# Half-length Fourier transform on folded rows, a rotation table built during the projection, and Toeplitz loads moved behind it

## What is computed

```
h = rms_norm(x, g_pre_mix) * (1 + sc_m) + sh_m
u, f, q, k, v = split(h @ w_in)
y_ssm = s5_mixer(u, ...)      # two complex linear scans, forward and backward, then GELU and a gate
y_fft = fourier_mixer(f, w_fft)
y_att = window_attention(q, k, v, sink)
y = concat(y_ssm, y_fft, y_att) @ w_out

def fourier_mixer(f, w_fft):
    ff = f.reshape(bsz, seq, FFT_HEADS, HEAD_DIM)
    mixed = fft2(ff, axes=(1, 3), norm='ortho').real
    return einsum('bshd,hde->bshe', mixed, w_fft)
```

## Time and profile before

| | |
|---|---|
| median of 3 runs | 3597.83 us |
| the three runs | 3597.83, 3578.83, 3598.26 us |
| profiled execution | 3580.67 us, its span 3578.9 us |
| PE busy | 3307.5 us (92% of the span) |
| DVE busy | 1477.8 us (41%) |
| ACT busy | 1020.0 us (29%) |
| mean granted TensorE clock | 0.963 of full speed |

### The profile page before, as it was taken

The page is one execution under the profiler, slowest core; times in us unless marked ns, Lnnn a source line. Parts: engine busy times, 40 slices in busy tenths (PEclk is TensorE's granted clock), DMA queues, the critical chain, the costliest instruction groups (busy, mean ns, idle before and its releaser), DMA issues.

```text
span 3578.9 us, 37529 instructions
## 1 busy us (share of the span) xinstructions
PE 3307.5 (92%) x14497; PEld 2571.8 (72%) x14497; DVE 1477.8 (41%) x2617; ACT 1020.0 (29%) x1475; POOL 217.8 (6%) x251
## 2 busy tenths in 40 slices
PE   6999788799999999999999998966888899999997
PEld 2575466688888788788888886754446688888885
DVE  6523642733443334411112354898543611111355
ACT  1111333523322232311121332314542312111231
POOL 4100210000000000000000001113330000000000
PEclk9899899899999999999999999987999999999998
DMA  8232003311111243211112343101003311111242
GB/s 279 96 58 100 11 8 112 100 47 47 47 52 48 76 135 119 81 53 47 47 47 65 108 132 96 36 24 34 1 0 113 117 47 47 49 51 47 94 141 100
DMA packets 245610, 260.35 MB, mean 73 GB/s; under 512 B 25680, under 2 KB 187464, under 8 KB 245396
## 3 DMA queue, kind: packets, MB, share of 16 engines
q1 hardware_dynamic: 235736, 253.05, 22.6%
q10 hardware_dynamic: 9788, 6.16, 0.6%
HBM read 237.55 MB, written 21.34 MB: 72 GB/s over the span
## 4 chain that ended last, share of the span: by engine, by line
PE 81%; DVE 10%; issue 4%; ACT 3%; ACTq 1%; DMA 0%; SPq 0%; POOL 0%; DVEq 0%
PE psum L942 40%; PE psum L797 25%; PE psum L2411 2%; PE psum L2440 2%; PE psum L1662 2%; DVE count_junk L1865 2%; PE psum L291 2%; PE psum L1642 1%; PE psum L1562 1%; PE psum L366 1%; DVE p L1930 1%; PE psum L335 1%; PE psum L1508 1%; PE psum L1652 1%; ACTq L2046 1%
## 5 line engine op out<-in xcount | busy, mean ns | idle before, releaser
L942 PE MATMUL psum<-x_hi,split_hi 128*128 128x512 f32 x2112 | 661.6, 391 | 14.7 <-DVE x_lo L1214 14.7
L942 PE MATMUL psum<-x_lo,split_hi 128*128 128x512 f32 x2112 | 660.7, 390 | 0.0
L942 PE MATMUL psum<-x_hi,split_lo 128*128 128x512 f32 x2112 | 660.3, 390 | 0.0
L942 PEld LDWEIGHTS psum<-x_hi,split_hi 128*128 128x128 f32 x2112 | 398.2, 189 | 99.5 <-DVE x_lo L1214 16.8
L942 PEld LDWEIGHTS psum<-x_hi,split_lo 128*128 128x128 f32 x2112 | 398.0, 188 | 82.9
L942 PEld LDWEIGHTS psum<-x_lo,split_hi 128*128 128x128 f32 x2112 | 398.1, 188 | 82.8
L797 PE MATMUL psum<-split_hi,src_hi 128*128 128x512 f32 x1312 | 406.6, 391 | 19.6 <-DVE split_lo L767 12.4
L797 PE MATMUL psum<-split_lo,src_hi 128*128 128x512 f32 x1312 | 405.5, 390 | 0.0
L797 PE MATMUL psum<-split_hi,src_lo 128*128 128x512 f32 x1312 | 405.1, 390 | 0.0
L848 DVE TENSOR_TENSOR split_lo<-raw,split_hi 128x1024 fp32r<-128x1024 f32 x132 | 160.8, 1220 | 564.4 <-ACT split_hi L844 564.4
L844 ACT CAST split_hi<-raw 128x1024 fp32r<-128x1024 f32 x132 | 138.7, 1052 | 604.5 <-PE psum L942 595.9
(11 more groups left out here) (393 smaller groups left out, 3594.5 us busy)
## 6 DMA issues: line engine op xcount, KB each, us to landing
raw<-in_ffn_w SPq DMA_DIRECT2D x176, 512.0 KB, 3.7
ada_w<-in_w_ada SPq DMA_DIRECT2D x12, 2048.0 KB
raw<-in_w_up SPq DMA_DIRECT2D x44, 512.0 KB, 3.7
raw<-in_w_down SPq DMA_DIRECT2D x44, 512.0 KB, 3.5
raw<-in_w_out SPq DMA_DIRECT2D x32, 512.0 KB, 3.5
res_dram<-hidden SPq DMA_DIRECT2D x32, 512.0 KB, 4.1
hidden<-res_dram SPq DMA_DIRECT2D x32, 512.0 KB, 5.2
dft_w<-in_dft SPq DMA_DIRECT2D x16, 512.0 KB, 3.7
```

Of the source, the lines that this page charges most:

```text
L942: ins = t.matmul(bank(4 * par + 2 * u + half), l[u][:, cols], r[:, k, HALF * half:HALF * (half + 1)], start=(k == 0 and m == 0), stop=(k = ...
```

## The change

1. **SP's order.** The eight loads `toep` move from ahead of units 4 to 9's loads to behind the Fourier tables and `att_bias`, where they wait for `uc_turned` (their new place is that of `u_rows`). `turn[0]` moves to the old place of `toep`.
2. **Folding.** Rows n and 1024-n of `f` meet the same cosine and opposite sines. `fold_fourier` on DVE, behind `split(4)`, writes their sum in the lower half of `f_t` and their difference in the upper half (six operations of 511 elements). Row 512 stands alone (`f_mid`).
3. **Mixing with `fw`.** Four blocks instead of eight, each by four 128-column matmuls instead of two of 256, and two with one output row for `f_mid`.
4. **Transform over positions.** The tables have 512 rows and 512 columns: four loads instead of 16, 16 matmuls of 512 columns instead of 64, even part and odd part in banks of their own. Two matmuls with one weight row (`dft_alt`) add row 512, and ten of two columns (`dft_alt_cols`) make output position 512. ACT copies the two odd banks, DVE adds and subtracts (the subtraction is written in reverse order).
5. **`turns(0)`** moves on DVE behind `split(5)`, in smaller pieces (at most 256 elements instead of 384). `turns(1)` stays, without the wait for `uc_turned`.

```diff
-    toep = place("toep", [P, CH, GROUPS * GC], RR + 16 * KB)
+    toep = place("toep", [P, CH, GROUPS * GC], RR)
...
-    turn = [place("turn", [P, 2, PAIRS, NCH], RR)[:], carry[1][:, :, :, 0:NCH]]
+    turn = [place("turn", [P, 2, PAIRS, NCH], RR + 16 * KB)[:], carry[1][:, :, :, 0:NCH]]
...
         sp.wait_ge(win_mm, Z_ALL)
-        for i in range(2 * NT):
-            if i >= 4:
-                sp.wait_ge(dft_mm, i - 3)
-            sp.dma_start(dft_w[i % 4][:], a["dft"][P * (i // 2):P * (i // 2 + 1), i % 2, :]).then_inc(dft_in[i % 4], 16)
+        for i in range(4):
+            sp.dma_start(dft_w[i][:], a["dft"][P * i:P * (i + 1)]).then_inc(dft_in[i // 2], 16)
+        sp.dma_start(dft_alt[:], a["dft_alt"]).then_inc(dft_in[1], 16)
+        sp.dma_start(dft_alt_cols[:], a["dft_alt_cols"]).then_inc(dft_in[1], 16)
         sp.wait_ge(u_turned, 6)
         sp.dma_start(att_bias[:], a["att_bias"]).then_inc(bias_in, 16)
+        sp.wait_ge(uc_turned, 6)
+        for s in range(CH):
+            sp.dma_start(toep[GC * s:GC * (s + 1), :, :],
+                         toep_dram[7 - s:15 - s].rearrange("t c n -> c t n")).then_inc(toep_in, 16)
...
         pe.wait_ge(fw_ready, 1)
-        for n in range(NT):
+        pe.wait_ge(f_folded, 1)
+        for n in range(4):
             if n >= 2:
                 pe.wait_ge(fm_ready, n - 1)
             for pair in range(2):
-                ins = t.matmul(bank(4 + n % 2, 2 * P, 2 * P * pair), f_t[:, pair, P * n:P * (n + 1)],
-                               fw[:, pair].rearrange("p c e -> p (c e)"), start=True, stop=True)
+                for cs in range(2):
+                    at_n = HALF * cs + P * n
+                    ins = t.matmul(bank(4 + n % 2, P, P * (2 * pair + cs)), f_t[:, pair, at_n:at_n + P], fw[:, pair, cs, :],
+                                   start=True, stop=True)
             ins.then_inc(fm_mm, 1)
+        pe.wait_ge(fm_ready, 3)
+        for pair in range(2):
+            ins = t.matmul(bank(4, P, P * pair)[0:1], f_t[:, pair, HALF:HALF + 1], fw[:, pair, 0, :], start=True, stop=True)
+        ins.then_inc(fm_mm, 1)
...
-            for pair in range(2):
-                for half in range(2):
-                    ins = t.matmul(bank(2 * pair + half), f_mixed[:, n, pair, cs, :], dft_w[i % 4][:, HALF * half:HALF * (half + 1)],
-                                   start=(i == 0), stop=(i == 2 * NT - 1))
-            ins.then_inc(dft_mm, 1)
-        pe.wait_ge(yf_ready, 4)
+                for cs in range(2):
+                    t.matmul(bank(2 * pair + cs), f_mixed[:, n, pair, cs, :], dft_w[n][:, cs, :],
+                             start=(n == 0), stop=(n == 3 and cs == 1))
+        for pair in range(2):
+            t.matmul(bank(2 * pair), f_mid[:, pair, :], dft_alt[:], start=False, stop=True)
+        for pair in range(2):
+            for n in range(4):
+                t.matmul(bank(6, 2, 2 * pair), f_mixed[:, n, pair, 0, :], dft_alt_cols[:], start=(n == 0), stop=False)
+            ins = t.matmul(bank(6, 2, 2 * pair), f_mid[:, pair, :], dft_alt_cols[0:1, :], start=False, stop=True)
+        ins.then_inc(dft_mm, 1)
+        pe.wait_ge(yf_ready, 3)
...
+        act.wait_ge(dft_mm, 1)
+        for pair in range(2):
+            s.copy(yf_odd[:, pair, :], bank(2 * pair + 1)).then_inc(yf_odd_ready, 1)
...
+            step = max(x for x in (3, 4, 6, PAIRS) if x * w <= (3 if d else 2) * NCH)
...
+    def fold_fourier(dve, v, steps):
+
+        dve.wait_ge(z_ready, Z_F)
+        for pair in range(2):
+            low, high, back = f_t[:, pair, 1:HALF], f_t[:, pair, HALF + 1:SEQ], f_t[:, pair, HALF + 1:SEQ][:, ::-1]
+            steps.add(v.tensor_tensor(f_diff[:, 1:HALF], low, back, ALU.subtract))
+            steps.settle()
+            steps.add(v.tensor_tensor(low, low, back, ALU.add))
+            steps.settle()
+            steps.add(v.tensor_copy(high, f_diff[:, 1:HALF]))
+            steps.settle()
+        dve.sem_inc(f_folded, 1)
...
+        for pair in range(2):
+            dve.wait_ge(yf_odd_ready, pair + 1)
+            even, odd = bank(2 * pair), yf_odd[:, pair, :]
+            steps.add(v.tensor_tensor(yc_t[:, 3 + pair, 0:HALF], even, odd, ALU.add))
+            ins = v.tensor_tensor(yc_t[:, 3 + pair, HALF + 1:SEQ][:, ::-1], even[:, 1:HALF], odd[:, 1:HALF], ALU.subtract)
+            ins.then_inc(yf_ready, 1)
...
-        sp.wait_ge(k_in_dram, 16 * 15)
-        for s in range(CH):
-            sp.dma_start(toep[GC * s:GC * (s + 1), :, :],
-                         toep_dram[7 - s:15 - s].rearrange("t c n -> c t n")).then_inc(toep_in, 16)
         for n in range(4, len(win_units)):
             sp.wait_ge(win_lo, n - 1)
             load_unit(n)
+        sp.wait_ge(k_in_dram, 16 * 15)
...
         for n in range(3, len(win_units)):
             split(n)
+            if n == 4:
+                fold_fourier(dve, v, steps)
+            elif n == 5:
+                turns(v, steps, 0)
```

More of the change, by code:

```diff
@@ L180, in body @@
     fw = place("fw", [P, 2, 2, P], RR + 42 * KB)
-    f_mixed = place("f_mixed", [P, NT, 2, 2, P], XR + 32 * KB)
-    dft_w = [place(f"dft_w{i}", [P, SEQ], XR + 4 * KB * i) for i in range(4)]
+    f_mixed = place("f_mixed", [P, 4, 2, 2, P], XR + 32 * KB)
+    f_mid = place("f_mid", [1, 2, P], XR + 40 * KB)
+    dft_w = [place(f"dft_w{i}", [P, 2, HALF], XR + 4 * KB * i) for i in range(4)]
+    dft_alt = place("dft_alt", [1, HALF], XR + 16 * KB)
+    dft_alt_cols = place("dft_alt_cols", [P, 2], XR + 18 * KB)
+    yf_odd = place("yf_odd", [P, 2, HALF], XR + 28 * KB)
+    f_diff = place("f_diff", [P, HALF], RR + 10 * KB)
     u_rows = place("u_rows", [P, GROUPS, CH, GC], RR)
@@ L199, in body @@
     probs = [place(f"probs{i}", [P, SPAN], at) for i, at in enumerate(probs_at)]
-    turn_tmp = [place(f"turn_tmp{i}", [P, 3, NCH], XR + 20 * KB + 1536 * i) for i in range(4)]
+    turn_tmp = [[place(f"turn_tmp{d}_{i}", [P, n], at + 4 * n * i) for i in range(4)]
+                for d, (n, at) in enumerate(((2 * NCH, RR + 8 * KB), (3 * NCH, XR + 20 * KB)))]
     probs_t = [place(f"probs_t{i}", [P, SPAN], RR + 40 * KB + 1536 * i) for i in range(2)]
@@ L207, in body @@
     fw_zero, fw_in, fw_mm, fw_ready = (sem(n) for n in ("fw_zero", "fw_in", "fw_mm", "fw_ready"))
[L208 to L209 removed]
+    fm_mm, fm_ready, dft_mm, yf_ready, yf_odd_ready = (sem(n) for n in ("fm_mm", "fm_ready", "dft_mm", "yf_ready", "yf_odd_ready"))
+    dft_in = [sem(f"dft_in{i}") for i in range(2)]
+    f_folded = sem("f_folded")
     u_turned, u_rows_ready, uc_turned, uc_ready = (sem(n) for n in ("u_turned", "u_rows_ready", "uc_turned", "uc_ready"))
@@ L394, in mix_scalar @@
         s.copy(fw[:].rearrange("p a c e -> p (a c e)"), bank(2)).then_inc(fw_ready, 1)
-        for n in range(NT):
+        for n in range(4):
             act.wait_ge(fm_mm, n + 1)
             s.copy(f_mixed[:, n].rearrange("p a c e -> p (a c e)"), bank(4 + n % 2)).then_inc(fm_ready, 1)
+        act.wait_ge(fm_mm, 5)
+        s.copy(f_mid[:].rearrange("o a e -> o (a e)"), bank(4, 2 * P)[0:1]).then_inc(fm_ready, 1)
         for i in range(6):
@@ L403, in mix_scalar @@
             s.copy(v_rows[:, 4 * i:4 * i + 4, :], bank(4 + i).rearrange("p (n c) -> p n c", n=4)).then_inc(v_ready, 1)
-        act.wait_ge(dft_mm, 2 * NT)
-        for i in range(4):
-            s.copy(yc_t[:, 3 + i // 2, HALF * (i % 2):HALF * (i % 2 + 1)], bank(i)).then_inc(yf_ready, 1)
+        act.wait_ge(dft_mm, 1)
+        for pair in range(2):
+            s.copy(yf_odd[:, pair, :], bank(2 * pair + 1)).then_inc(yf_odd_ready, 1)
+        s.copy(yc_t[:, 3:5, HALF:HALF + 1], bank(6, 4).rearrange("p (a c) -> p a c", a=2)[:, :, 0:1]).then_inc(yf_ready, 1)
         def exponentials(n, part):
@@ L570, in sums @@
             v.reciprocal(att_sum[:, of_block(n)], att_sum[:, of_block(n)]).then_inc(sums_ready, 1)
-        dve.wait_ge(uc_turned, 6)
-        for d in range(2):
-            turns(d)
+        turns(v, steps, 1)
         steps.add(v.tensor_scalar(by_head(sink_neg[:]), sink_row[:].rearrange("p (e j) -> p j e", e=2), -1.0, None, ALU.mult))
-        dve.wait_ge(yf_ready, 4)
+        for pair in range(2):
[4 more added lines that the diff above has]
+            ins.then_inc(yf_ready, 1)
         steps.add(v.memset(carry[0][:, :, :, 0:1], 0.0))
@@ L2480, in constants @@
     turn_d = 2 * np.pi / HEAD * ((m[:, None] * m[None, :]) % HEAD)
-    dft = np.stack([np.cos(turn), np.sin(turn)], 1) / 32.0
+    dft = np.stack([np.cos(turn), np.sin(turn)], 1)[0:SEQ // 2, :, 0:SEQ // 2] / 32.0
+    alternate = (1.0 - 2.0 * (n[0:SEQ // 2] % 2)) / 32.0
     eye2 = np.eye(2)
@@ L2491, in constants @@
         "dft": dft.astype(np.float32),
+        "dft_alt": alternate[None, :].astype(np.float32),
+        "dft_alt_cols": np.repeat(alternate[0:P, None], 2, 1).astype(np.float32),
         "dft_d": dft_d.astype(np.float32),
```

57 lines of the change are left out of this document (26 added, 31 removed).

## The result

The changed kernel takes 3538.95 us in the median of four runs (3532.46 to 3546.81) and the kernel before 3595.52 beside it (3578.83 to 3598.26): a ratio of 0.985, 95% interval 0.981 to 0.989. Repeated on another occasion, unaltered: 3545.06 (five runs, 3537.33 to 3548.06) against 3586.96 (nine runs), ratio 0.988 (0.986 to 0.990). So the gain is 57 us by the first comparison, 42 by the second. The profiled executions lie 47.5 us apart (spans 3578.9 and 3531.4).

A forecast was written before the change was run, and what follows sets the result against it. TensorE carries 81% of the chain; outside the feed-forward layers its waits and removable work count. Gains 7.0 + 2.9 + 35.9 = 45.8 us take 3597.8 to 3552.0 us (profiled execution 3580.67 to 3534.9); range 3527 to 3565.

The forecast's parts named there:

- Term 1: SP's order in the projection: unit 4's load comes earlier, PE's gap and the slow matmuls behind it go; gain 7.0 us.
- Term 2: Folding and mixing: folds hidden on DVE, mixing takes 4.4 us instead of 7.26; gain 2.9 us.
- Term 3: Transform over positions, first matmul to first states: 21.3 us instead of 57.2; gain 35.9 us.
- Term 4: Tables on DVE: `turns(1)` hidden by almost 8 us, `turns(0)` before `split(6)` with 1.7 us over; cost 0.
- Rival A: Clock falls ahead of the attention and stays low in more of the loop: 3554 to 3556 us, chance 0.2.
- the likeliest case: The forecast itself, gain 45.8 us to 3552.0 us, holding the rest of the chances, 0.56.
- the signs named for "wrong": PE waiting at 242, twenty small records over 4 us, first states of 2.8 us, or attention loop longer than 140 us.
- B: Projection's gap stays because unit 4's load is late for another reason: 38.8 us gained, 3559 us, chance 0.07.
- C: `turns(0)` is late for `split(6)` in the projection, PE waits 1.6 us: 3553.6, or 3556 us; chance 0.12.
- D: Little of the transform's gain arrives, as `toep`, `att_bias` or `turn` was due at the old time: 3559 us, chance 0.04.

The follow-up runs named there:

- the filler: Four extra 512-column matmuls into a free bank behind the column products, covering the wait for the sums, against the changed kernel: 3538.36 us (four runs), ratio 0.9882.
- the new order: Changed kernel with the transform's small products first, then odd banks, then even ones: 3549.97 us (four runs), ratio 0.9921.
- the few columns: Changed kernel with eight of the ten two-column products left out, output position 512 wrong: 3529.37 us, one execution.
- the late table: Changed kernel with `turns(0)` back behind the `u_rows` copies, next to `turns(1)`: 3552.26 us (five runs), ratio 0.9919; repeat, a single run, 3554.34.
- the late split: Changed kernel with ten more idle DVE operations between `turns(0)` and `split(6)`: 3544.46 us, one execution.

## Why the prediction was right

The forecast was 3552.0 us from the shown median, and 3534.9 for the counterpart of the profiled execution; measured 3538.95 and 3533.17. The range held both medians (3538.95 and 3545.06). Up to the first states the sum says 45.8 us and the profiles 45.3.

- **Term 1, 7.0 us: as predicted.** No pause at 220, a load at 203.68, PE busy 32.00 of 32.00. The last pair starts 8.5 us earlier; 1.5 of it had arisen before 196 us, in code that both have. Alone it was 6.9. (Two slips that change nothing: the projection's end was given as 285.6, where 7.0 off makes 285.9, and came at 284.4; the moved loads' "12 us at most" should be 12.6.)
- **Term 2, 2.9 us: wrong in size in the profiled execution, by the clock.** The mixing took 5.9 us, not 4.4. The records were right: in four other profiles with the same products up to there (the filler, the new order, the few columns, the late table) the 32 records ran in 3.8 us at full clock, which makes 4.3 with those of one output row. In the changed kernel, its repeat and the late split the clock fell in this stretch. The chain's gain there was 1.3 instead of 2.9. That the sum still came out to 0.5 us at the states is luck in part: these 1.6 us and the 1.5 of term 1 that no edit brought cancel. Of the 47.5 us between the spans, 3.3 come from untouched code behind the product with the logits.

```profile
286.00:296.00 10.00, 8.99 (x59) 8.13 (x58) 1.66 (x3) 3.23 (x6) 0.00 (x0) 0.83 0.56 203
```

- **Term 3, 35.9 us: right.** 21.64 us against 21.3; measured parts: 13.89 (13.8), 1.91 (2.1), 2.7 for the two-column ones (2.2), the first odd copy 0.6 (0.6), the four sums 2.5 (2.5), hand-overs 0.1 (0.1).
- **Term 4, 0: right.** The first table ran 16.27 us (16.3), `split(6)` ended with 1.8 us to spare (1.7 predicted), and the late split put a price on the far side of it.
- **Rival A came true as a mechanism, inside the likeliest case's total.** The granted clock was 0.50 at the first states, which took 1.3 us more (2.83). I had given it 0.2. In all six profiles that have the whole wait for the sums in them, the first states ran at half speed behind thin work and the wait (2.83 us). The Trainium skill ("TensorE: Matmul & The Clock Gate", section "HAM oscillation — how this bites in real kernels") says of a kernel whose bursts of matmuls are parted by waits that the clock drops in them and each next burst starts slow. These six agree, and 0.2 looks too low; the old kernel's 2.14 us wait does not settle it, with 1.53 us behind it in two profiles and 2.83 in a third. Two of the signs named for "wrong" came with it: states of 2.83 us, and a loop of 141.2 us instead of 139.7. At the readers of `toep` the lead is 43.8 us: 45.3 less 1.5, a little under the 1.7 to 3.4 at which rival A was priced.
- **Rivals B, C and D did not happen.** The late split shows C's price; the late table shows what D would have cost for `turn`.
- **The median** was forecast 13 us too high. The step that failed was to take the difference off a median of three runs. Over all 38 runs of the kernel before in these comparisons the median is 3580.3 and the highest 3603.6, so 3597.8 was a high draw; the changed kernel's nine have 3544.7. The gain between these is 35.6 us (the 38 come from four occasions, on two of which the changed kernel did not run), between the lowest runs 41.8, between the profiled executions 47.5. The 44 us at the readers of `toep` are what the change does up to there; what a total adds or takes is the draw of later stages. It is not an even draw: 20 of the 34 executions of the kernel before whose clock is on record had a mean of 0.963 or more, 2 of the changed kernel's nine. So the changed kernel loses time in later, unedited code more often than the old one did; why was not tested.

## What to carry to other kernels

Price a shorter computation by its matmul records and by what then stands behind it: halving twice the products (64 to 16) paid 35.6 of 57.2 us, but it also took away DVE's cover, and without the table's new place 7.7 us of it would have gone again. Compare two kernels where the edited code ends, not only at the end of the span, when later stages at a changing clock move the total by 10 to 20 us; but look at the totals too, since here the changed kernel ran its later stages at the lower clock more often than the old one. Ask of a median from three runs which group it fell into.

## What the runs showed of the hardware

- The clock is not settled by the program. The same program kept 1.00 through the logits in one execution and dropped to 0.50 in another (257.5 and 269.6 us for the product around them). In programs that differ elsewhere, the same matmuls ran at either clock too: the mixing (32 records in 3.8 or 5.4 us), and the states behind the old transform's 2.14 us wait (24 records in 1.53 or 2.83 us).
- PE being busy does not keep it up: 0.50 with 2.00 of 2.00 us busy behind two-column products, and 0.50 with 8.89 of 10.00 in matmuls over 64 rows, where 8.33 of 10.00 had gone with 1.00 in the other execution.
- A float32 product of two columns costs 0.25 us (eight records in 0.98), one with a single weight row and 512 columns 0.96, against 0.87 over 128 rows: products with next to no arithmetic are far from free.
